# Gated delta rule of two layers: exponentials of the decays ahead of the last SiLUs, the keys' products right behind the norms, k and v turned two heads at a time inside the levels

## What is computed

```python
decay = jnp.exp(jnp.where(causal, gcum[..., :, None] - gcum[..., None, :], -jnp.inf))
kb = kc * bc[..., None]
m = jnp.where(strict, jnp.einsum('nbhid,nbhjd->nbhij', kb, kc) * decay, 0.0)
t_inv = lax.linalg.triangular_solve(eye + m, jnp.broadcast_to(eye, m.shape), left_side=True, lower=True)
u = t_inv @ (vc * bc[..., None])
w = t_inv @ (kb * jnp.exp(gcum)[..., None])
qk = jnp.einsum('nbhid,nbhjd->nbhij', qc, kc) * decay
def step(state, inp):
    u_i, w_i, qk_i, qd_i, kd_i, gl_i = inp
    v_new = u_i - w_i @ state
    o_i = qd_i @ state + qk_i @ v_new
    state = state * gl_i[..., None, None] + jnp.swapaxes(kd_i, -1, -2) @ v_new
    return state, o_i
```

## Time and profile before

| | us |
|---|---|
| median of 3 runs | 2988.69 |
| lowest and highest | 2985.67, 2990.87 |
| profiled execution, its own time | 2994.42 |
| its span, first to last instruction | 2992.6 |
| busy: TensorE matmul, TensorE weight load | 2847.6, 2534.4 |
| busy: VectorE, ScalarE, GpSimd | 2080.7, 1456.0, 149.0 |
| mean granted TensorE clock | 0.968 of full |

### The profile page before, as it was taken

One profiled execution on the slowest core, in us unless ns is written; L12 is line 12 of the kernel. 1 busy time (PEld: TensorE's weight loads), 2 busy tenths in 40 slices (PEclk: granted clock), 3 DMA queues, 4 the chain that ended last, 5 costly groups with the idle time before them and its releaser, 6 DMA issues.

```text
span 2992.6 us, 53944 instructions
## 1 busy us (share of the span) xinstructions
PE 2847.6 (95%) x22916; PEld 2534.4 (85%) x22916; DVE 2080.7 (70%) x3259; ACT 1456.0 (49%) x1957; POOL 149.0 (5%) x257
## 2 busy tenths in 40 slices
PE   5999999999999999999899999999999999999998
PEld 5888899978888888998788877889788888887887
DVE  5986757758878867576686577764676668658674
ACT  2545644545445455445454355544554345435553
...
GB/s 260 258 249 166 114 74 212 181 115 240 243 207 265 243 156 113 98 205 179 113 230 182 157 153 100 197 183 174 95 197 183 172 154 209 184 200 74 153 182 102
DMA packets 516703, 521.43 MB, mean 174 GB/s; under 512 B 16503, under 2 KB 513728, under 8 KB 516464
## 3 DMA queue, kind: packets, MB, share of 16 engines
...
## 4 chain that ended last, share of the span: by engine, by line
PE 83%; DVE 9%; ACT 5%; issue 2%; DMA 1%; ACTq 0%; POOL 0%; SPq 0%; DVEq 0%; POOLq 0%
PE P L65 81%; DVE wsp L74 4%; ACT wsp L71 2%; PE P L68 1%; ACT arena L71 1%; DVE arena L74 1%; DVE arena L82 1%; DVE ACC L82 1%; DMA raw<-in_nsa_w_in 1%; DVE X L74 1%; ACT L71 0%; ACT HX L71 0%; DVE HX L82 0%; DVE X L82 0%; DMA raw<-in_ada_w 0%
## 5 line engine op out<-in xcount | busy, mean ns | idle before, releaser
L65 PE MATMUL P<-HX,wsp 128*128 128x256 f32 (+1 forms) x10304 | 1621.6, 319 | 40.4 <-DVE wsp L74 14.1
L65 PEld LDWEIGHTS P<-HX,wsp 128*128 128x128 f32 x10304 | 1462.0, 193 | 179.4 <-issue 22.7
L74 DVE TENSOR_TENSOR wsp<-raw,wsp 128x2048 fp32r<-128x2048 f32 (+4 forms) x440 | 946.2, 2152 | 375.1 <-ACT wsp L71 374.6
L71 ACT ACTIVATE wsp<-raw 128x2048 fp32r<-128x2048 f32 (+4 forms) x440 | 790.8, 1799 | 551.0 <-PE P L65 494.1
L65 PE MATMUL P<-FG,wsp 128*128 128x256 f32 (+1 forms) x2816 | 496.1, 337 | 1.6 <-DVE wsp L74 1.6
L65 PEld LDWEIGHTS P<-FG,wsp 128*128 128x128 f32 x2816 | 428.6, 188 | 64.9 <-DVE wsp L74 2.9
L71 ACT ACTIVATE arena<-P 128x512 f32<-128x512 f32 (+3 forms) x384 | 214.6, 569 | 542.8 <-PE P L65 542.0
L74 DVE TENSOR_TENSOR arena<-arena,P 128x512 f32<-128x512 f32 (+2 forms) x232 | 151.1, 653 | 188.5 <-ACT arena L71 155.0
L65 PE MATMUL P<-arena 64*64 64x64 f32 (+9 forms) x4000 | 241.4, 263 | 17.6 <-ACT arena L71 9.9
...
L82 DVE SCALAR_TENSOR_TENSOR ACC<-raw,sm,ACC 128x256 f32<-128x256 f32 x476 | 230.8, 485 | 16.7
L65 PE MATMUL P<-GX,wsp 128*128 128x256 f32 (+1 forms) x1592 | 228.6, 303 | 7.6 <-DVE GX L74 7.6
...
## 6 DMA issues: line engine op xcount, KB each, us to landing
...
```

The source lines that it names most:

```text
L65: return self if self.e is None else self.e.matmul(*a, skip_group_check=True, **k)
L71: return self if self.e is None else self.e.activation(*a, **k)
L74: return self if self.e is None else self.e.tensor_tensor(*a)
```

## The change

- **Order on ScalarE.** `conv_act` ends with the last tile's three copies. The split that stood behind them and the SiLUs of tiles 10 and 11 now stand in `delta_act` behind all eight exponentials.
- **Order on TensorE.** The 32 keys' products come right behind the 16 decay products, ahead of the spreads. Level 0's x products follow, then the identity starts. k and v are turned by transposes of 128 x 128, one for two heads: eight per chunk (four of k, four of v), chunk s behind the x products of level s, for levels 0 to 3.
- **Order on VectorE.** The last split is made in level 1. Taps 11 are made in two halves among the products with the masks, all keys' ahead of the queries'. KT and KD are made in levels 0 to 3, qe in levels 4 and 5. The reduction steps are dealt out as 5, 1, 5, 5, 5 and then all that are left (11).
- **Modulation products.** The first two stand in levels 3 and 4 and no longer in 2 and 3; the third stands behind `un(1)`, and its sum on VectorE behind the first state.
- **Layout.** `QKV` is stored by pairs of heads, then chunk, then head, so that two heads of a chunk are 128 adjacent columns (`CHUNKS` is a view of it); MKQ, XX and KD lie elsewhere.

The diff, cut to its core:

```diff
-    QKV = ar(0, 24, 256)
+    QKV = ar(0, 6144).rearrange("p (r c q j) -> p r q c j", r=12, c=4, q=2)
+    CHUNKS = ar(0, 6144).rearrange("p (a r c q j) -> p r c q a j", a=3, r=4, c=4, q=2)
...
             ins.then_inc(*CVA.up((l, i)))
+            if i == 11:
+                return
...
                 e.activation(HN[:, 16:32], P[bank["qksum", l]][:, 16:32], ACT.Sqrt, bias=EPSC).then_inc(*HNR.up((l, "qk")))
-        conv_silu_act(e, l, 11)
     def conv_silu_act(e, l, i):
-        v = QKV[:, 2 * i:2 * i + 2, :]
+        v = QKV[:, i]
         e.wait_ge(*TAP.at((l, i)))
-        e.activation(v, v3(CT[i % 2], 2), ACT.Silu).then_inc(*SIL.up((l, i)))
+        e.activation(v, chunks(CT[i % 2]), ACT.Silu).then_inc(*SIL.up((l, i)))
...
                 e.wait_ge(*CSUM.at((l, i - 2)))
-            e.activation(SQ2[i % 2], v, ACT.Square).then_inc(*SQQ.up((l, i)))
+            e.activation(SQ2[i % 2].rearrange("p q (c j) -> p q c j", c=4), v, ACT.Square).then_inc(*SQQ.up((l, i)))
...
                 taps_dve(e, l, i - 1)
-            ready_dve(e, U["qkv", l][i])
+            if i < 11:
+                ready_dve(e, U["qkv", l][i])
...
     def unit_dve(e, l, j):
-        v = QKV[:, 2 * j:2 * j + 2, :]
+        v = QKV[:, j]
         e.wait_ge(*CSPR.at((l, j)))
-        e.tensor_tensor(v, v, v3(P[bank["unit", l, j]][:, :], 2), ALU.mult).then_inc(*ULN.up((l, j)))
+        e.tensor_tensor(v, v, chunks(P[bank["unit", l, j]][:, :]), ALU.mult).then_inc(*ULN.up((l, j)))
...
-    MKQ = [ar(6144 + 512 * c, 2, 4, 64) for c in range(4)]
-    XX = [ar(8192 + 256 * c, 4, 64) for c in range(4)]
+    MKQ = [ar(13312 + 512 * c, 2, 4, 64) for c in range(4)]
+    XX = [ar(6144 + 256 * c, 4, 64) for c in range(4)]
     UT = [ar(9216 + 512 * c, 2, 4, 64) for c in range(4)]
-    KT, KD, VT = ([ar(o + 512 * c, 4, 128) for c in range(4)] for o in (11264, 13312, 15360))
+    KT, KD, VT = ([ar(o + 512 * c, 4, 128) for c in range(4)] for o in (11264, 7168, 15360))
...
     WT = [[ar(18944 + 1024 * t + 512 * q, 2, 4, 64) for q in range(2)] for t in range(2)]
-    O = QKV[:, 16:24, :]
+    O = ar(4096, 8, 256)
...
                 give((l, "dd", 2 * t + r), DAC.at((l, "dd", 2 * t + r)))
+        e.wait_ge(*ULN.at((l, 7)))
+        for c in range(4):
+            b = take(e, (l, "qk", c))
+            for hp, q in both():
+                x = CHUNKS[:, hp, c, q]
+                ins = e.matmul(v3(P[b][half(q), 128 * hp:128 * hp + 128], 2), x[:, 1, :], x[:, 0:2, :], start=True, stop=True)
+            ins.then_inc(*DMM.up((l, "qk", c)))
+            give((l, "qk", c), DVC.at((l, "m", c)), DVC.at((l, "qd", c)))
...
                 give((l, "eb", 2 * t + r), DAC.at((l, "eb", 2 * t + r)))
-        e.wait_ge(*ULN.at((l, 7)))
-        qk = QKV[:, 0:16, :].rearrange("p (a h) s -> p h a s", a=2)
-        for c in range(4):
-            b = take(e, (l, "qk", c))
-            for hp, q in both():
-                h = 2 * hp + q
-                ins = e.matmul(v3(P[b][half(q), 128 * hp:128 * hp + 128], 2), QKV[:, 8 + h, chunk(c)], qk[:, h, :, chunk(c)],
-                               start=True, stop=True)
-            ins.then_inc(*DMM.up((l, "qk", c)))
-            give((l, "qk", c), DVC.at((l, "m", c)), DVC.at((l, "qd", c)))
-        for c in range(4):
-            b = take(e, (l, "ut", c))
-            for q in range(2):
-                i64 = ident[half(q), half(q)]
-                e.matmul(v3(P[b][half(q), :], 8), i64, i64.unsqueeze(1).broadcast_to([64, 8, 64]), start=True, stop=False)
-        for name, row in (("kt", 8), ("vt", 16)):
-            for c in range(4):
-                b = take(e, (l, name, c))
-                if name == "vt":
-                    e.wait_ge(*SIL.at((l, 11)))
-                for hp, q in both():
-                    ins = e.matmul(P[b][half(q), 128 * hp:128 * hp + 128], QKV[:, row + 2 * hp + q, chunk(c)], ident, start=True, stop=True)
-                ins.then_inc(*DMM.up((l, name, c)))
-                if name == "kt":
-                    give((l, name, c), DVC.at((l, "kd", c)))
-                else:
-                    give((l, name, c), DAC.at((l, "v", c)))
...
+        def turned(name, c):
...
+            b = take(e, (l, name, c))
+            for hp in range(4):
+                w = 512 * (hp + (4 if name == "kt" else 8)) + 128 * c
+                ins = e.transpose(P[b][:, 128 * hp:128 * hp + 128], arena[:, w:w + 128], ident)
+            ins.then_inc(*DMM.up((l, name, c)))
+            give((l, name, c), DVC.at((l, "kd", c)) if name == "kt" else DAC.at((l, "v", c)))
...
                 give((l, "x", s, c), DVC.at((l, "x", s, c)))
-            if 2 <= s < 5:
-                ada_pe(e, delta_ada(l)[s - 2])
+            if s == 0:
+                for c in range(4):
+                    b = take(e, (l, "ut", c))
+                    for q in range(2):
+                        i64 = ident[half(q), half(q)]
+                        e.matmul(v3(P[b][half(q), :], 8), i64, i64.unsqueeze(1).broadcast_to([64, 8, 64]), start=True, stop=False)
+                e.wait_ge(*SIL.at((l, 11)))
+            if s < 4:
+                turned("kt", s)
+                turned("vt", s)
+            if s in (3, 4):
+                ada_pe(e, delta_ada(l)[s - 3])
...
         un(1)
+        ada_pe(e, delta_ada(l)[2])
...
     def delta_act(e, l):
-        e.wait_ge(*SIL.at((l, 11)))
...
             e.activation(EB[c].rearrange("p h j -> p (h j)"), P[bank[l, "eb", c]][:, :], ACT.Exp).then_inc(*DAC.up((l, "eb", c)))
-        for c in range(4):
-            e.wait_ge(*DMM.at((l, "vt", c)))
-            for hp in range(4):
-                ins = e.activation(VT[c][:, hp, :], P[bank[l, "vt", c]][:, 128 * hp:128 * hp + 128], ACT.Copy, scale=pair_col(BB, c, hp))
-            ins.then_inc(*DAC.up((l, "v", c)))
+        for i in (10, 11):
+            conv_silu_act(e, l, i)
+        ready_act(e, U["qkv", l][11])
...
             n = 512 if s < 5 else 256
+            if s < 4:
+                e.wait_ge(*DMM.at((l, "vt", s)))
+                for hp in range(4):
+                    ins = e.activation(VT[s][:, hp, :], P[bank[l, "vt", s]][:, 128 * hp:128 * hp + 128], ACT.Copy, scale=pair_col(BB, s, hp))
+                ins.then_inc(*DAC.up((l, "v", s)))
...
         for c in range(4):
+            if c % 2 == 0:
+                taps_dve(e, l, 11, (c // 2,))
...
             e.wait_ge(*DMM.at((l, "qk", c)))
-            e.wait_ge(*DPL.at((l, "mq", c)))
+            e.wait_ge(*DPL.at((l, "m", c)))
             e.tensor_tensor(MKQ[c][:, 0], v[:, 1], MKQ[c][:, 0], ALU.mult).then_inc(*DVC.up((l, "m", c)))
+        for c in range(4):
+            v = P[bank[l, "qk", c]][:, :].rearrange("p (h a j) -> p a h j", h=4, a=2)
+            e.wait_ge(*DPL.at((l, "q", c)))
...
         e.wait_ge(*GVC.at((l, "bx")))
-        for c in range(4):
-            kt = v3(P[bank[l, "kt", c]][:, :], 4)
-            e.wait_ge(*DMM.at((l, "kt", c)))
-            e.wait_ge(*DMM.at((l, "eb", 1)))
-            e.tensor_tensor(KT[c], kt, pair_cols(BX, c).broadcast_to([128, 4, 128]), ALU.mult).then_inc(*DVC.up((l, "kt", c)))
-            e.tensor_tensor(KD[c], kt, pair_cols(EK, c).broadcast_to([128, 4, 128]), ALU.mult).then_inc(*DVC.up((l, "kd", c)))
         steps = [(j, q) for j in delta_ada(l) for q in range(8)]
+        first = 0
         for s in range(6):
-            if 3 <= s:
-                mod_dve(e, delta_ada(l)[s - 3])
+            if 4 <= s:
+                mod_dve(e, delta_ada(l)[s - 4])
...
                 e.tensor_tensor(XX[c], x, level(s), ALU.mult).then_inc(*DVC.up((l, "x", s, c)))
-            if s == 0:
-                for c in range(4):
-                    qe = QKV[:, 0:8, chunk(c)]
+            if s < 4:
+                kt = v3(P[bank[l, "kt", s]][:, :], 4)
+                e.wait_ge(*SIL.at((l, 11)))
+                e.wait_ge(*DMM.at((l, "kt", s)))
+                e.wait_ge(*DMM.at((l, "eb", 1)))
+                e.tensor_tensor(KT[s], kt, pair_cols(BX, s).broadcast_to([128, 4, 128]), ALU.mult).then_inc(*DVC.up((l, "kt", s)))
+                e.tensor_tensor(KD[s], kt, pair_cols(EK, s).broadcast_to([128, 4, 128]), ALU.mult).then_inc(*DVC.up((l, "kd", s)))
+            else:
+                for c in (2 * s - 8, 2 * s - 7):
+                    qe, eb = CHUNKS[:, :, c, :, 0, :], EB[c].rearrange("p (r q) j -> p r q j", q=2)
                     e.wait_ge(*DAC.at((l, "eb", c)))
-                    e.tensor_tensor(qe, qe, EB[c], ALU.mult).then_inc(*DVC.up((l, "qe", c)))
-            for j, q in steps[6 * s:6 * s + 6]:
+                    e.tensor_tensor(qe, qe, eb, ALU.mult).then_inc(*DVC.up((l, "qe", c)))
+            if s == 1:
+                ready_dve(e, U["qkv", l][11])
+            n = 1 if s == 1 else 5
+            for j, q in steps[first:first + n]:
                 ada_step(e, j, q)
+            first += n
+        for j, q in steps[first:]:
+            ada_step(e, j, q)
...
         state(0)
+        mod_dve(e, delta_ada(l)[2])
```

13 lines of the change are left out of this document (7 added, 6 removed).

## The result

The changed kernel takes 2964.8 us (median of 4 runs, 2964.06 to 2965.97) against 2987.47 of the kernel before beside it: 22.7 us less, a ratio of 0.9928 with a 95% interval of 0.9916 to 0.994. The forecast was 2974.3 with a range down to 2966; the time lies 1.2 us under it. The profiled execution took 2964.7, its span 2962.9.

A forecast was written before the change was run, and what follows sets the result against it. TensorE's own work was taken as the bound, with 7.2 us of idleness and a slow clock behind it in the front. 24.8 - 6.0 + 1.1 - 3.8 - 1.7 = 14.4 us gained, so 2974.3 us; range 2966 to 2982.

The forecast's parts named there:

- Steps 1 and 2: Before level 0: exponentials ahead of SiLUs and split; keys' products behind the norms after 1.4 us idle, taking 3.4 us.
- Step 3: Before level 0: GpSimd masks and VectorE taps alternate, six pairs taking 6.75 us; front 18.0 us, 24.8 us gained in all.
- Clock: TensorE's clock falling after the new gaps: 1.7 us lost in all, between ends of 0 and 6.8 us.
- The longer wait I feared: TensorE's gap of about 3.2 us ahead of level 0, 351.75 to 354.95, that might lower the clock.
- Step 4: Levels 1 to 3: transposes of two heads, 1.0 us per turned pair, now inside the levels; 6.0 us given back.
- Step 5: VectorE's work in the levels makes TensorE wait nowhere; the wait behind level 0 goes, 1.1 us gained in two layers.
- Step 6: Behind level 5: VectorE's longer list stalls the fourth new-value products 1.9 us per layer, 3.8 us lost.
- Free engines: Rival before level 0: GpSimd and VectorE don't hold each other up, no clock fall; 22.0 us gained, 2966.7 us; chance 0.22.
- Transposes that don't overlap their loads: Rival in turning keys and values: each transpose costs a load of 0.11 us more, 7.1 us; 2981.4 us; chance 0.10.
- Less than it says: Rival: early exponentials only move the wait, clock falls, VectorE late in two levels; 7.3 us gained, 2981.4 us; chance 0.10.
- slower: Rival in the levels: clock stays down 20 us per layer, 3.9 us lost, 2992.6 us; chance 0.03.
- the two ends of Step 3: Level 0's first products end at 356.55 if GpSimd and VectorE alternate, 353.6 if they run freely; the first was taken.

## Why the prediction was wrong

Direction and mechanisms held; the sum came out too small: 14.4 us of gain forecast, 22.7 measured.

- **Steps 1 and 2 held.** Exponentials from 343.88; a wait of 1.36 us for the norms (1.4 forecast); keys' products at full clock, 3.64 us (3.4). By the runs that put parts back, the early exponentials hold 5.6 to 5.9 us of a layer's front and the split 3.1 to 3.2, the clock that falls without them included; the two were not put back together. The order of keys' products and spreads, which I never priced by itself, costs 1.25. What it is worth that k and v are turned inside the levels has no run of its own.
- **Step 3 is the step that failed, by a size.** The mechanism, GpSimd's masks and VectorE's taps in each other's way, is there: the run without queries' masks shows it. The term was mis-sized: six pairs in series at 1.125 us, 2.95 us of delay for TensorE, where 0.80 to 0.83 us per tap and a wait of 1.01 and 0.94 us were measured. I had taken whole instructions as exclusive ("it waits for the whole split"). The row itself said less: the addition grew by 2.87 - 0.74 = 2.13 us beside a split of 2.29, 0.15 us less than the split still had to go. And the other addition there, of 0.74 us, was not by itself as I wrote (the figure stands; one at 566.87 takes 0.74 with VectorE all but idle): 0.09 us behind its start VectorE began a split, and this time the split grew:

```profile
568.31 2.80 DVE L74 TENSOR_TENSOR wsp<-raw,wsp 128x2048 fp32r<-128x2048 f32 x1 [0.17 <-ACT wsp L71]
```

By 2.80 - 2.29 = 0.51 us beside the 0.65 that were left of the addition, again 0.15 less. So in either order the later of the two pays, and some 0.15 us of an instruction hold nobody up. On one of 2.29 us that is small; on a tap of 0.49 it is a third. An estimate from these two rows alone is 0.49 + 0.635 - 2 x 0.15 = 0.83 us a pair, and 0.55 with half masks of 0.36, where 0.80 to 0.83 and 0.53 to 0.56 were measured. Six pairs took 2.50 + 2.40 = 4.90 us instead of the 6.75 forecast. The Trainium skill (SBUF — State Buffer, "SBUF: two separate sides") speaks of the whole instruction too; the runs agree on who meets whom, and not on the length, 0.83 us a pair instead of 1.125. The front gave 14.5 + 13.4 = 27.9 us instead of 24.8.

- **Clock, the second failed term.** 1.7 us forecast for the two stretches, none lost in them: the waits were 1.36, 1.01 and 1.57 us, and the clock is 1.00 in both profiles of the changed kernel. The row it came from (0.72 at 434 us) shows a fall behind the start of the z gates, which comes in some executions of both kernels and says nothing of the new waits. The longer wait I feared, 3.2 us, was a consequence of Step 3's size.
- **Step 4 held:** 1.03 us per turned pair, 6.2 given back (6.0). **Step 5 held:** no wait on VectorE in levels 1 to 5, 1.1 won. **Step 6** held as mechanism, its size a little off: waits of 1.57 and 1.58 instead of 1.9, 3.2 us lost instead of 3.8.
- **Sum of the measured terms:** 27.9 - 6.2 + 1.1 - 3.2 = 19.6. TensorE's gaps put down to nothing account for 2.2 more (3.8 us in the two stretches before, 1.6 after; 2.5 and 1.2 in the repeats), with -0.4 left over to the 21.3 of the stretches. They were a term of the old kernel that the prediction left at nothing; by the repeats it is 1.3 and not 2.2.

**The rivals.** *Free engines* gave the nearer time, 2966.7, and that by luck: the engines are not free, the delay left over is small, and the gaps that nobody had counted make up for it. *Transposes that don't overlap their loads* is refuted by the run with products. *Less than it says* and *slower* did not come: no wait took the place of the exponentials', and the clock in the levels is 1.00. The range was too narrow at its low end, because I took the two ends of Step 3 as bounds and left no room for the gaps, which no term covered.
